# Up projections with tokens as the stationary operand, their results brought to features on partitions by 32x32 squares and five transfers

## The reference

```python
def causal_depthwise_conv(x, w, b):        # K = 3 here
    xp = jnp.pad(x, ((0, 0), (K - 1, 0), (0, 0)))
    y = b
    for k in range(K):
        y = y + xp[:, k:k + S] * w[k]
    return y

def conv_ffn(h, w_up, conv_w, conv_b, w_down):       # w_up: 2048 x 11264, w_down: 5632 x 2048
    u = causal_depthwise_conv(h @ w_up, conv_w, conv_b)
    val, gate = jnp.split(u, 2, axis=-1)
    return (jax.nn.gelu(gate) * val) @ w_down
...
        x = x + conv_ffn(rms_norm(x, ffn_norm[layer]), ffn_w_up[layer], ...)
```

## Time and profile before

| | |
|---|---|
| three timed runs | 2302.14, 2302.88 (median), 2303.87 us |
| the profiled execution: its own time | 2301.86 us |
| its span, first to last instruction | 2300.2 us |
| busy, share of the span | PE 100%, PEld 86%, DVE 68%, ACT 55%, POOL 8% |
| granted TensorE clock | 1.000 |
| DMA | 429.10 MB, mean 187 GB/s |

### The profile page before, as it was taken

One profiled execution on the slowest core, in us unless ns is written; L12 is line 12 of the kernel. 1 busy time (PEld: TensorE's weight loads), 2 busy tenths in 40 slices (PEclk: granted clock), 3 DMA queues, 4 the chain that ended last, 5 costly groups with the idle time before them and its releaser, 6 DMA issues.

```text
span 2300.2 us, 37299 instructions
## 1 busy us (share of the span) xinstructions
PE 2292.3 (100%) x12832; PEld 1988.9 (86%) x12832; DVE 1559.9 (68%) x1945; ACT 1263.6 (55%) x1709; POOL 189.7 (8%) x171
## 2 busy tenths in 40 slices
PE   9999999999999999999999999999999999999999
PEld 7888888998888888888888888899888888888887
DVE  6766766577777777755556778658877777774443
ACT  6645665466555555544444776556555555553333
POOL 0810002130000000000000100213000000000000
PEclk9999999999999999999999999999999999999999
DMA  8656435455565555565555555646665555556555
GB/s 277 208 188 206 136 120 184 164 165 187 179 200 188 186 187 187 192 195 187 188 191 183 177 189 181 198 131 195 220 198 186 186 188 187 194 178 204 195 193 165
DMA packets 119714, 429.10 MB, mean 187 GB/s; under 512 B 13856, under 2 KB 14752, under 8 KB 119632
## 3 DMA queue, kind: packets, MB, share of 16 engines
q1 hardware_dynamic: 117696, 420.40, 55.8%
q0 software_dynamic: 1792, 7.52, 1.0%
q10 hardware_dynamic: 144, 0.06, 0.0%
HBM read 423.73 MB, written 2.10 MB: 185 GB/s over the span
## 4 chain that ended last, share of the span: by engine, by line
PE 99%; ACT 0%; DVE 0%; issue 0%; DMA 0%; SPq 0%; ACTq 0%
PE ps L360 46%; PE ps L364 23%; PE ps L402 15%; PE ps L407 7%; PE ps L345 2%; PE ps L381 2%; PE ps L697 1%; PE ps L923 1%; PE ps L683 0%; PE ps L777 0%; PE ps L666 0%; PE ps L605 0%; PE ps L659 0%; PE ps L798 0%; DMA xT<-in_x_t 0%
## 5 line engine op out<-in xcount | busy, mean ns | idle before, releaser
L333 DVE TENSOR_TENSOR w_lo<-raw,w_hi 128x1024 fp32r<-128x1024 f32 x788 | 969.2, 1236 | 549.2 <-ACT w_hi L327 546.3
L327 ACT ACTIVATE w_hi<-raw 128x1024 fp32r<-128x1024 f32 x787 | 827.0, 1056 | 617.8 <-PE ps L364 359.4
L360 PE MATMUL ps<-xg_hl,w_hi 128*128 128x512 f32 x3328 | 1046.4, 396 | 0.0
L364 PEld LDWEIGHTS ps<-xg_hl,w_lo 128*128 128x128 f32 x3328 | 625.2, 188 | 147.8
L364 PE MATMUL ps<-xg_hl,w_lo 128*128 128x256 f32 x3328 | 653.8, 278 | 0.0
L360 PEld LDWEIGHTS ps<-xg_hl,w_hi 128*128 128x128 f32 x3328 | 506.9, 189 | 0.2
L360 PE MATMUL ps<-a_hl,w_hi 128*128 128x512 f32 x960 | 301.5, 395 | 0.0
L402 PE MATMUL ps<-w_hi,a_hl 128*128 128x512 f32 x952 | 238.1, 392 | 0.3 <-ACT vmem L1053 0.2
L364 PEld LDWEIGHTS ps<-a_hl,w_lo 128*128 128x128 f32 x960 | 180.3, 188 | 42.6
L402 PEld LDWEIGHTS ps<-w_hi,a_hl 128*128 128x128 f32 x952 | 176.6, 188 | 37.5 <-issue 0.7
L364 PE MATMUL ps<-a_hl,w_lo 128*128 128x256 f32 x960 | 188.6, 278 | 0.0
(11 more groups left out here) (208 smaller groups left out, 1732.0 us busy)
## 6 DMA issues: line engine op xcount, KB each, us to landing
raw<-in_w_stream SPq DMA_DIRECT2D x787, 512.0 KB, 3.6
bias<-in_rel_bias POOLq DMA_DIRECT2D x4, 768.0 KB, 5.7
memT<-in_mem_t POOLq DMA_DIRECT2D x4, 512.0 KB, 6.6
gate_w<-in_gate_w POOLq DMA_DIRECT2D x4, 512.0 KB, 3.9
x_tok<-x_turned SPq DMA_DIRECT2D x16, 128.0 KB, 3.6
out_t<-x_tok SPq DMA_DIRECT2D x8, 256.0 KB, 4.2
xT<-in_x_t SPq DMA_DIRECT2D x2, 512.0 KB, 7.2
xT<-in_x_t SPq DMA_DIRECT2D x3, 256.0 KB, 7.8
```

Of the source, the lines that this page charges most:

```text
L327: nc.scalar.activation(w_hi[:, s, :], raw[:, s, :], ACT.Copy).then_inc(hi_done, 1)
L333: nc.vector.tensor_tensor(w_lo[:, s, :], raw[:, s, :], w_hi[:, s, :].bitcast(F), ALU.subtract).then_inc(lo_done, 1)
L360: nc.tensor.matmul(ps[:, bank + m, :], w_hi[:, s, w], both, start=start and k == ks[0], stop=False, skip_group_check=True)
L364: last = nc.tensor.matmul(ps[:, bank + m, SEQ:2 * SEQ], w_lo[:, s, w], x[:, xk, 0, :], start=False, stop=stop and k == ks[-1], skip_group_ ...
```

## The change

Up units become token units: block `half` 0 of an iteration (8 units) makes 512 gate columns, block 1 the 512 value columns, for both 128-token tiles, in two PSUM banks each (4 and 5, 6 and 7). Now tokens lie on partitions, and 1/rms is a scale for each partition: the row `r_bc` and PE's four matmuls for it go. For every block: ACT copies two banks out with the scale (`up_tiles`, into `y_up`), DVE turns them in 32x32 squares (`up_turn`, two transposes into `z_t`), SP stores `z_t` to memory (`keep`, 128 x 1088 floats) and loads it back in four transfers of 32 partitions (`moves`, into `u_t`, in which features are on partitions and the tokens lie in four runs of 64), and POOL copies the two last tokens of each run ahead of the next (`halos`). Then come the taps, four tiles at a time, with gelu, product and splits. `y_up` and `u_t` are one place. The weights' columns and the token order of `xg_hl` are permuted to fit. `x_turned` also goes by way of memory: one store of 2 MB and four loads of 512 KB. The diff, cut to its core:

```diff
-WOVEN = [("x", 0), ("x", 1), ("x", 2), ("x", 3), ("x", 4), ("u", 0), ("x", 5), ("x", 6), ("u", 4), ("x", 7), ("u", 1), ("u", 5),
-         ("u", 2), ("u", 6), ("u", 3), ("u", 7)]
...
+WOVEN = [("x", 0), ("x", 1), ("x", 2), ("x", 3), ("x", 4), ("u", 0), ("x", 5), ("u", 1), ("x", 6), ("u", 2), ("x", 7), ("u", 3),
+         ("u", 4), ("u", 5), ("u", 6), ("u", 7)]
+U_UP = 2 * (KT // 2)
+VALUE_AT, GATE_AT = 4, 12
+HALO, RUN = 4, 4 + CHUNK
+UP_ITER = FT // 4
+MOVES = 4 * 16
...
-        u_buf = sb("u_buf", [4, SEQ + 2])
-        y_buf = sb("y_buf", [4, SEQ])
+        UT, ZT = FFN, FFN + size([4, 4, RUN])
+        u_t = sb("u_t", [4, 4, RUN])
+        z_t = sb("z_t", [4, 4, RUN])
+        y_up = at("y_up", UT, [TT, COLS])
...
+        z_home = nc.dram_tensor("z_home", (P, 4, 4 * RUN), F, kind="Internal").ap()
+        x_home = nc.dram_tensor("x_home", (P, 4, TT * COLS), F, kind="Internal").ap()
...
-            x_moved = first["up1"] + 6 * SLOTS
...
+            def up_units(l):
+                c0 = first[f"up{l}"] + 2 * SLOTS
+                def keep(i, half):
+                    sp.wait_ge(zt_ready, times(TT * (2 * l * UP_ITER + half + 1), i, 2 * TT))
+                    sp.dma_start(z_home, z_t[:, :, :, :].rearrange("p b k n -> p b (k n)")).then_inc(z_kept, 16)
+                def moves(i, half, bs):
+                    sp.wait_ge(z_kept, times(16 * (2 * l * UP_ITER + half + 1), i, 2 * 16))
+                    for b in bs:
+                        sp.dma_start(u_t[SQ * b:SQ * b + SQ, :, :, :].rearrange("p a k n -> p a (k n)"),
+                                     z_home[:, b, :].rearrange("(a j) n -> j a n", a=4)).then_inc(ut_in, 16)
+                def x_moves(bs):
+                    sp.wait_ge(x_kept, 16)
+                    for b in bs:
+                        sp.dma_start(x_tok[SQ * b:SQ * b + SQ, :, :, :].rearrange("p c t n -> p c (t n)"),
+                                     x_home[:, b, :].rearrange("(c i) n -> i c n", c=4)).then_inc(x_tok_in, 16)
+                def body(i, x_at=False):
+                    for u in range(U_UP):
+                        sp.wait_ge(lo_done, times(c0 + u - SLOTS + 1, i, U_UP))
...
+                        if u in (7, 15):
+                            keep(i, u // 8)
+                        if u in (9, 10):
+                            moves(i, 0, (2 * (u - 9), 2 * (u - 9) + 1))
+                        if u in (1, 2) and i is not None:
+                            moves(i, -1, (2 * (u - 1), 2 * (u - 1) + 1))
+                        if x_at and u == 3:
+                            sp.wait_ge(xz_ready, len(X_TURNS))
+                            sp.wait_ge(xsq_ready, SQ_BEFORE["xo1"] + N_BLOCKS)
+                            sp.dma_start(x_home, x_turned[:, :, :, :, :].rearrange("p a t k j -> p a (t k j)")).then_inc(x_kept, 16)
+                        if x_at and u in (5, 6):
+                            x_moves((2 * (u - 5), 2 * (u - 5) + 1))
+                body(None)
+                body(1, l == 1)
+                with sp.Fori(2, UP_ITER) as i:
+                    body(i)
+                after = first[f"up{l}"] + N_UP + 2 * SLOTS
+                sp.wait_ge(lo_done, after - SLOTS + 1)
+                unit(0, after)
+                moves(UP_ITER, -1, range(4))
+                for s in range(1, SLOTS):
+                    sp.wait_ge(lo_done, after + s - SLOTS + 1)
+                    unit(s, after + s)
...
-                        q, u = j // U_BLOCK, j % U_BLOCK
...
-                        pair_unit(pe, first[f"xo{l}"] + pos, 4 * u, xg_hl, UP_BANK[q], u == 0, u == U_BLOCK - 1, ready=up_there)
-                    if pos == 12:
+                        if j == 0:
+                            pe.wait_ge(proj_free, fblock[f"xo{l}"] + 2 + 1 + 1)
+                        token_unit(pe, first[f"xo{l}"] + pos, 2 * j, 2, xg_hi, xg_lo, UP_BANK[0], j == 0, j == 7, up_there)
+                    if pos == 13:
                         stats_pe(pe, (FFN0, FFN1)[l])
-                bcast_pe(pe, (FFN0, FFN1)[l])
             def up_section(l):
...
+                c0 = first[f"up{l}"]
                 def body(i):
-                    for u in range(2 * U_BLOCK if i is None else 0, 4 * U_BLOCK):
-                        q, k = u // U_BLOCK, 4 * (u % U_BLOCK)
...
-                        pair_unit(pe, c0 + u, k, xg_hl, 2 * (q % 2), k == 0, k == KT - 4, i, 4 * U_BLOCK)
+                    for half in range(1 if i is None else 0, 2):
+                        if i is None:
+                            pe.wait_ge(proj_free, fblock[f"xo{l}"] + 2 + 3 + 1)
+                        else:
+                            pe.wait_ge(up_out, times(TT * (2 * l * UP_ITER + half - 1), i, 2 * TT))
+                        for u in range(8):
+                            token_unit(pe, c0 + 8 * half + u, 2 * u, 2, xg_hi, xg_lo, UP_BANK[half], u == 0, u == 7, None, None, i, U_UP)
                 body(None)
-                with pe.Fori(1, FT // 4) as i:
+                with pe.Fori(1, UP_ITER) as i:
                     body(i)
...
+            def up_tiles(l, i, half):
+                b = 2 * l * UP_ITER + half
+                act.wait_ge(pe_unit, times(first[f"up{l}"] + 8 * (half + 1), i, U_UP))
+                if i is not None or b:
+                    act.wait_ge(conv_done, times(4 * b, i, 8))
+                for tt in range(TT):
+                    A(y_up[:, tt, :], ps[:, UP_BANK[half] + tt, :], ACT.Copy, scale=r_tok[:, (FFN0, FFN1)[l], tt:tt + 1]).then_inc(up_out, 1)
+            def taps(l, i, back, half, tiles):
+                b = 2 * (l * UP_ITER - back) + half
+                act.wait_ge(ut_in, times(MOVES * (b + 1), i, 2 * MOVES))
+                for m in tiles:
+                    w = 4 * (4 * (1 - half) + m) - 32 * back
+                    A(chunks(y_tile(half, m - 4 * back, i)), u_t[:, :, m, HALO:RUN], ACT.Identity, scale=column(fconv, w + 2, i, 32),
+                      bias=column(fconv, w + 3, i, 32)).then_inc(tap_done, 1)
+            def gate_gelu(l, i):
+                act.wait_ge(conv_done, times(8 * l * UP_ITER + 4, i, 8))
...
+            def value_hi(l, i, back):
+                act.wait_ge(g_ready, times(l * UP_ITER - back + 1, i, 1))
+                A(pair_tiles(a_hi, -4 * back, 4, i, 4), pair_tiles(y_hl[:, :, 1, :], -4 * back, 4, i, 4), ACT.Copy).then_inc(g_hi, 1)
...
+                c0 = first[f"up{l}"]
+                def body(i):
+                    for u in range(8 if i is None else 0, U_UP):
+                        split_hi(act, c0 + u + SLOTS, i, U_UP)
+                        if u < 10 and i is not None:
+                            value_slot(l, i, u)
+                        if u % 8 == 7:
+                            up_tiles(l, i, u // 8)
+                        if u in (GATE_AT, GATE_AT + 1):
+                            x = 2 * (u - GATE_AT)
+                            taps(l, i, 0, 0, (x, x + 1))
+                        if u == GATE_AT + 2:
+                            gate_gelu(l, i)
...
+            def up_turn(l, i, half):
+                b = 2 * l * UP_ITER + half
...
+                for tt in range(TT):
+                    dve.wait_ge(up_out, times(TT * b + tt + 1, i, 2 * TT))
+                    V.transpose(z_t[:, :, :, HALO:RUN].rearrange("p b k (i t) -> p t (b k) i", t=TT)[:, tt, :, :],
+                                y_up[:, tt, :].rearrange("p (c j) -> p c j", j=SQ)).then_inc(zt_ready, 1)
+            def conv(l, i, back, half, tiles):
+                b = 2 * (l * UP_ITER - back) + half
+                if tiles[0] == 0:
+                    dve.wait_ge(halo_done, times(b + 1, i, 2))
+                for j, count in ((1, mid_done), (0, conv_done)):
+                    for m in tiles:
+                        dve.wait_ge(tap_done if j else mid_done, times(4 * b + m + 1, i, 8))
+                        y = chunks(y_tile(half, m - 4 * back, i))
+                        V.scalar_tensor_tensor(y, u_t[:, :, m, HALO - 2 + j:RUN - 2 + j], column(fconv, 4 * (4 * (1 - half) + m) - 32 * back + j, i, 32),
+                                               y, ALU.mult, ALU.add).then_inc(count, 1)
+            def product(l, i, back):
...
+            def value_lo(l, i, back):
+                dve.wait_ge(g_hi, times(l * UP_ITER - back + 1, i, 1))
...
+            def value_slot(l, i, u):
+                if isinstance(i, int) and i == UP_ITER:
+                    if u == VALUE_AT:
+                        conv(l, i, 1, 1, range(4))
+                    if u == VALUE_AT + 1:
+                        product(l, i, 1)
+                    if u == VALUE_AT + 2:
+                        value_lo(l, i, 1)
+                    return
+                if u in (VALUE_AT, VALUE_AT + 1):
+                    x = 2 * (u - VALUE_AT)
+                    conv(l, i, 1, 1, (x, x + 1))
+                if u == VALUE_AT + 2:
+                    product(l, i, 1)
+                if u == VALUE_AT + 4:
+                    value_lo(l, i, 1)
...
```

(17 more changed lines are left out.)

299 lines of the change are left out of this document (120 added, 179 removed).

## The result

The changed kernel takes 2362.98 us (median of 4, 2359.19 to 2367.23) against 2303.20 for the one before (2302.14 to 2303.87): ratio 1.0261, 95% interval 1.024 to 1.0281. It is slower by 60 us where 25 less were forecast. Of the rivals "the same loop, and slower than before" came true in its time, though not in the place that it named. The profiled execution took 2359.19, which is 82.3 above the 2276.9 of the sum.

The account below looks back on a forecast made before the run. PE's own pace was taken as the bound: token units 23.7 us and the spread row 1.3 made 25.0, so profiled 2301.9 becomes 2276.9, median 2277.9; range 2275.5 to 2288.

Parts of the forecast that it names:

- the same loop, and slower than before: Rival: `up_tiles` waiting for the taps makes the kernel slower by over 0.2% from R = 13.0; chance 0.07.
- Pace of PE: Up units at 2.720 us, not 2.787: 11.3 a layer, plus woven units 1.1, spread row 1.3; 25.0 us in all.
- The loop through memory: Turns of a value and a gate block, 10.4 + R and 9.2 + R, fit in 43.5 us; price nothing.
- R: Time from the last transpose to `u_t` being there: forecast 9.3 us, allowed up to 11.9.
- The store, 3.6: Store of 557 KB to memory within R, taken as 3.6 us like a 512 KB load.
- The rival built on the Trainium skill's rule of a slow receipt at memory: The slower-loop rival, chance 0.07: semaphores wait for the target's receipt and memory is the slowest target.
- Outside R, 10.4 + 9.2: Loop work besides R: 10.4 us for a value block's turn, 9.2 for a gate block's.
- slowest sum: R with the slowest store, 5.3 + 2.1 + 3.6 = 11.0 us; the slower-loop rival's R = 13.5 lies 2.5 beyond.
- The price 40 x (R - 11.9) - 14: Slower-loop rival's cost in us: eats 25.0 at R = 12.9, takes 50 back at R = 13.5, giving 2328.
- `y_up` and `u_t` are one place: Reason given for the loop: `up_tiles` of a block waits for all taps of the block before.
- Queue and x turn: Added 49 MB raises DMA share from 0.57 to about 0.63; `x_home` delays weights in `up1`; nothing, bounds 0 and 3.
- Sum of squares: POOL's squares ahead of PE's L419 have 1.0 us of cover: nothing, or up to 1 for both layers.

Follow-up runs that it names:

- e16_together: Against the changed kernel: all four `u_t` loads in one step of SP, no weight load between the second and third; 2281.93 us, ratio 0.9915.
- e1_own: Against the changed kernel: `y_up` gets a place of its own, so `up_tiles` need not wait for the taps that read `u_t`; 2360.61 us, ratio 1.0252.

## Why the prediction was wrong

- **Pace of PE, 25.0 us: right.** Units follow each other in 2.72 us. In e16_together the first `a_hl` matmul of `down0` starts at 966.78, 12.6 before 979.34, where 11.3 + 0.6 + 0.65 make 12.5; its profiled execution took 2278.95, 2.0 above the sum.
- **The loop through memory: the mechanism right, the size wrong.** The step that failed is "with one load of weights between them, so the last goes out 2.1 after the first and lands 3.6 later". The last was out 2.4 us after the first (613.66 to 616.02), but a load's time was taken from L526 in a kernel whose DMA engines were busy for 0.57, with nothing put down for the bytes that stand ahead of it. Here 544 KB of loads, with 512 KB of weights among them, were in the queue together, and the DMA share beside them is full. A stretch of the changed kernel with the loads under way, and the next but one:

```profile
616.00:620.00 4.00, 4.00 (x20) 3.30 (x19) 0.79 (x1) 0.00 (x0) 0.00 (x0) 1.00 1.06 249
...
624.00:628.00 4.00, 3.65 (x16) 3.04 (x17) 4.00 (x9) 2.56 (x5) 0.00 (x0) 1.00 0.22 66
```

  The mean share over an up section, 0.74, hides that it swings between 1.06 and 0.22. 512 KB at the 249 GB/s of the first row would be 2.1 us, an estimate; 2.3 was measured (8.9 less 6.6). So the loads term of R was 5.7 for 8.9: 2.3 for the weights among them, 0.9 for the queue in general.
- **The store, 3.6:** 4.4 us to the first load's issue, 0.8 of the 4.0 us that R was off. The rival built on the Trainium skill's rule of a slow receipt at memory gets no support from it: in the same kernel a weight load of 512 KB takes 4.1 us to landing, the store of 544 KB 4.2, where 3.6 were taken for both. What grew is the time of either kind.
- **Outside R, 10.4 + 9.2:** 21.1, 1.5 more. After the gate block's taps copies and transposes take 2.6 (629.58 to 632.15), not 1.9, since DVE has a split in the way; the other 0.8 was not traced, and the prediction had counted ten hand-overs at nothing. So the bound was R of 11.2, not 11.9: (43.5 less 21.1) / 2. The forecast's R of 9.3 would still have fitted, the "slowest sum" of 11.0 just so, which is where e16_together stands.
- **The price 40 x (R - 11.9) - 14:** with the right bound 40 x (13.3 - 11.2) is 84, less 14 is 70; measured 82.3. One turn in `up1`, the one beside the x turn, adds about 7 more (below, at the x turn). The last 5 are not traced to a place. Seen from PE, the 82 are 54 us more of idle time than before and 28 more of busy time than the sum has (last section); that is the same loss, not a second one. The slope of 40 was about right, and it made an error of 4 us in R one of 80 in time.
- **What closes the loop:** "`y_up` and `u_t` are one place" was not enough as a reason (e1_own); the order of instructions on ACT and DVE closes it too. The sum of one turn is the same.
- **Chance 0.07:** the slowest case was summed from the largest rows of a kernel whose queue was emptier. That is no upper bound once the change itself adds 49 MB to that queue in bursts.
- **Queue and x turn:** the DMA share was 0.74 in `up0`, not near 0.63. The prediction had spread the added 149 us of all engines over the whole span; they fall in the two up sections, 468 us each before, where they make 0.16 and not 0.06, and 0.57 + 0.16 is 0.73. For the x turn "nothing, bounds 0 and 3" holds in e16_together, where PE waits once for 1.6 us, but not in the changed kernel. There the store beside it was read back 14 us after its issue, behind the x turn's transfers, and that turn of the loop took 30.6 us (1663.48 to 1694.04) where the gate blocks beside it take 23.7:

```profile
1663.48 0.34 SPq L542 DMA_DIRECT2D z_home<-z_t  x1
...
1677.42 0.80 SPq L548 DMA_DIRECT2D u_t<-z_home  x2
...
1694.04 0.33 SPq L542 DMA_DIRECT2D z_home<-z_t  x1
```

  The same turn is as late in e16_together, where PE bore it but for the 1.6 us:

```profile
1623.93 0.50 SPq L542 DMA_DIRECT2D z_home<-z_t  x1
1625.31 2.60 SPq L496 DMA_DIRECT2D raw<-in_w_stream  x2
1637.97 1.75 SPq L548 DMA_DIRECT2D u_t<-z_home  x4
```

- **Sum of squares:** no wait of PE there.

Left open: how the 0.9 us of the loads that are late even with nothing among them divides between their own bytes and the weights ahead of them, and the last 5 us of the 82.

## What to carry to other kernels

Where a change closes a loop through transfers, write down the loop's time against the time that it may take, and price the transfers with what stands ahead of them in the queue, not by a lone transfer's row: in these runs the bytes that were issued first were served first, whoever needed them. The order of issues in one queue was worth more here than the number, size, source or engine of the transfers; issuing two of four small loads ahead of a weight load, and not behind it, gave back 79 us (2363.0 less 2283.5). And near the bound of a loop a microsecond counts once for each turn, so the range of a forecast has to be that of the term times the turns.

## What was unexpected in the hardware

A wait of PE of some 2 us can be followed by a stretch at half the clock. In the changed kernel PE idles at 740.7 to 743.4 for `w_hi`, and the matmuls behind it take 3.59 us, where 1.98 is usual:

```profile
737.86 1.98 PE L413 MATMUL ps<-w_hi,xg_hl 128*128 128x512 f32 x8
739.67 1.07 PE L418 MATMUL ps<-w_lo,xg_hl 128*128 128x512 f32 x4
743.35 3.59 PE L413 MATMUL ps<-w_hi,xg_hl 128*128 128x512 f32 x8 [2.61 <-ACT w_hi L338]
```

Windows of 4 us around the same thing 100 us later; the third figure from the end is the granted clock as a part of 2.4 GHz:

```profile
836.00:840.00 4.00, 0.72 (x3) 0.57 (x3) 1.86 (x5) 2.76 (x5) 0.24 (x1) 0.84 0.36 141
840.00:844.00 4.00, 4.00 (x11) 3.13 (x10) 4.00 (x7) 2.16 (x3) 0.00 (x0) 0.50 0.37 131
844.00:848.00 4.00, 4.00 (x15) 3.19 (x15) 3.30 (x4) 3.02 (x4) 0.00 (x0) 0.81 0.62 184
```

PE had waited for 3.3 us of the first; the clock is then at its lower level, 1.2 GHz, throughout the second, which costs 2.0 us, and for two fifths of the third. After the wait of 0.85 at 624.35 it stayed at 1.00. The length of a wait does not decide it alone: after 2.5 us of waiting up to 648.9 the clock did not fall, as the next row shows, while after 2.15 us up to 981.4 it did.

```profile
648.00:652.00 4.00, 3.07 (x13) 2.55 (x14) 4.00 (x9) 3.76 (x5) 0.00 (x0) 1.00 0.08 20
```

PE's busy time is 2295.2 here and 2268.5 in e16_together, for the same matmuls, 27 us more. About half of it is the clock: its mean is 0.994 over 2357.4 us, against 1.000, which is 14 us. The rest was not looked into. It is no loss of its own in this kernel. The loop sets the length of the section, and PE does not lengthen the loop: the stretch from landing to the last transpose takes 10.98 us in the value block beside the wait at 740.7 as it does in those without a slow stretch; with a full clock PE would only have waited longer for its next split.
